# Sum of squares of the first RMSNorm: summed by VectorE, multiplied once with ones, in a kernel for a hybrid decoder layer

## The reference, cut to what matters

```
def rms_norm(x, g):
    y = xf * lax.rsqrt(jnp.mean(xf * xf, axis=-1, keepdims=True) + EPS)
    return (y * g.astype(jnp.float32)).astype(x.dtype)
...
h = rms_norm(xp, g_mix[l])
q, k, v, qi, ki, wi, p, ga, gb = project(h, w_in[l])
```

## Time and profile before

| | us |
|---|---|
| median of 3 runs | 1686.36 |
| lowest, highest | 1683.05, 1686.56 |
| profiled execution, its own time | 1681.07 |
| span of its trace | 1679.6 |
| TensorE busy in the span | 1620.0 (96%) |
| VectorE, ScalarE, GpSimd busy | 599.3, 303.6, 204.9 |

### The profile page before, as it was taken

How to read it: one execution, slowest core, us unless ns; L and a number is a source line. 1 busy time by engine, 2 the same in 40 slices (tenths; PEclk the granted TensorE clock), 3 DMA queues, 4 the chain that set the end, 5 groups by cost and what they waited for, 6 DMA issues and landing times. The chain is left out here.

```text
span 1679.6 us, 33459 instructions
## 1 busy us (share of the span) xinstructions
PE 1620.0 (96%) x13803; PEld 767.0 (46%) x13803; DVE 599.3 (36%) x1168; ACT 303.6 (18%) x617; POOL 204.9 (12%) x267
## 2 busy tenths in 40 slices
PE   7999999999999599999999999999999999999995
PEld 6678577786755233333333333333333333333331
DVE  3409837702323432333233323332333233323333
ACT  1300020006312012111111121111111211121112
POOL 3612400005200000000000000000000000000000
PEclk9899999999999699999999999999999999999996
DMA  4553754722272399999999999999999999999963
GB/s 167 186 169 125 259 198 163 244 78 114 68 298 96 144 375 404 398 399 387 404 391 399 391 401 394 398 384 399 393 400 386 403 395 400 389 399 392 396 248 112
DMA packets 70504, 510.00 MB, mean 304 GB/s; under 512 B 11310, under 2 KB 11758, under 8 KB 45230
## 3 DMA queue, kind: packets, MB, share of 16 engines
q1 hardware_dynamic: 60070, 485.28, 72.9%
q0 software_dynamic: 10384, 24.06, 6.1%
HBM read 491.61 MB, written 22.37 MB: 306 GB/s over the span
## 5 line engine op out<-in xcount | busy, mean ns | idle before, releaser
L1160 PE MATMUL PS<-weight_ring,region_experts 128*32 128x512 f32 x6144 | 680.5, 595 | 2.9 <-issue 1.7
L1160 PEld LDWEIGHTS PS<-weight_ring,region_experts 128*32 128x32 f32 x6144 | 198.7, 110 | 415.4 <-issue 412.0
L822 PE MATMUL PS<-region_x,region_w 128*128 128x260 f32 (+1 forms) x1056 | 240.7, 388 | 2.2 <-ACT region_x L657 1.0
L1167 PE MATMUL PS<-weight_ring,act_turned 128*32 128x512 f32 x2048 | 232.2, 594 | 0.0
L822 PEld LDWEIGHTS PS<-region_x,region_w 128*128 128x128 f32 x1056 | 200.7, 191 | 39.0 <-issue 4.1
L1462 DVE TENSOR_TENSOR region_experts<-region_experts,region_x 128x640 bf16<-128x640 f32 x33 | 27.2, 825 | 397.2 <-DMA region_experts<-b_gu 396.8
L1167 PEld LDWEIGHTS PS<-weight_ring,act_turned 128*32 128x32 f32 x2048 | 63.3, 110 | 137.7 <-issue 134.0
L608 POOL DMA_INDIRECT y_acc<-region_x,idx_i x32 | 46.7, 1460 | 640.6 <-issue 640.6
L1173 PE MATMUL PS<-weight_ring,act_turned 128*32 128x256 f32 x2048 | 122.2, 379 | 0.0
L1173 PEld LDWEIGHTS PS<-weight_ring,act_turned 128*32 128x32 f32 x2048 | 66.6, 110 | 71.2 <-issue 38.3
L592 POOL DMA_INDIRECT region_x<-h_rows,idx_i x33 | 33.4, 1013 | 440.7 <-DVE idx_i L1476 427.6
(11 more groups left out here) (254 smaller groups left out, 1242.1 us busy)
## 6 DMA issues: line engine op xcount, KB each, us to landing
weight_ring<-w_gu SPq DMA_DIRECT2D x128, 2048.0 KB, 13.9
weight_ring<-w_down SPq DMA_DIRECT2D x64, 2048.0 KB, 16.5
region_w<-w_mt SPq DMA_DIRECT2D x33, 512.0 KB, 4.3
weight_ring<-cache_kT SPq DMA_DIRECT2D x64, 256.0 KB, 4.0
weight_ring<-cache_v SPq DMA_DIRECT2D x64, 256.0 KB, 4.0
weight_ring<-w_out SPq DMA_DIRECT2D x2, 2048.0 KB, 11.1
weight_ring<-bias_strip SPq DMA_DIRECT2D x1, 2560.0 KB, 12.6
region_x<-xT SPq DMA_DIRECT2D x4, 536.0 KB, 7.1
```

Source lines behind the costliest of these rows:

```text
L822: mm = pe.matmul(PB[j % 2][:, a, 0:width], lhs(k), rhs(k)[:, width * a:width * a + width], start=(k == 0), stop=(k == nk - 1))
L1160: mm = pe.matmul(out[GRP * j:GRP * j + GRP], hTe[:, k, GRP * g:GRP * g + GRP], weights(c)[:, k, :], start=(k == 0), stop=(k == KD - 1))
L1167: pe.matmul(bank(3)[GRP * j:GRP * j + GRP], actT[:, k, GRP * g:GRP * g + GRP], w_dn[:, k, 512 * q:512 * q + 512], start=(k == 0), stop=(k ...
```

## The change

VectorE adds the eight tiles of sq into one tile ss of 128 x 536 (seven additions), each pair of additions right behind the two xw products of the same pair of tiles. TensorE multiplies ones with ss alone (two products instead of 16), into PSUM banks 4 and 5 (SS) instead of PB[0]. It is no job any more: all job numbers fall by one, so qi0 is job 0. ScalarE computes one root of a 1-column tile right after its squares, so that its table for the root is loaded then. TensorE does twelve products ones x ones into bank 7 before anything else. Item 4 is issued ahead of SP's wait for hT, item 5 ahead of the value weights.

```
--- before.py
+++ after.py
@@ -153,6 +153,7 @@
 
         x_in = part(X1, 0, KD, NT)
         sq = part(X2, 0, KD, NT)
+        ss = part(W6, slot(4) + 1024, NT)
         hT = part(X1, 0, KD, NT)
         xw = part(W6, slot(3), KD, NT)
 
@@ -272,6 +273,7 @@
         DB = [AB[0], AB[1], PSF[:, 0:1024], PSF[:, 1024:2048]]
         PTB = [bank(2), bank(3)]
         RX = bank(1)
+        SS = PS[:, 4:6, :]
         PTR = [PSF[32 * n:32 * n + META, 5 * 512:5 * 512 + P] for n in range(2)]
         L_g = [bank(4, 256), bank(5, 256)]
         L_n = [bank(6, 1)[0:32], bank(7, 1)[0:32]]
...
@@ -300,10 +302,10 @@
         scat = [sem(f"scattered{n}") for n in range(2)]
 
 
-        J_SS, J_QI, J_KI, J_WI, J_K, J_Q, J_P, J_V, J_MIX, J_GATE = 0, 1, 5, 6, 7, 11, 15, 19, 24, 28
+        J_QI, J_KI, J_WI, J_K, J_Q, J_P, J_V, J_MIX, J_GATE = 0, 4, 5, 6, 10, 14, 18, 23, 27
 
         zq_v = zq[:, 0:1032].rearrange("p (c x) -> p c x", x=258)
-        J_A, J_WO = 52, 60
+        J_A, J_WO = 51, 59
 
         N_MT = 17
         ITEMS = N_MT + 3 * KD + KD
@@ -367,10 +369,12 @@
             sp.dma_start(bias_new, bias_n).then_inc(S["small_in"], 16)
             sp.dma_start(cst[:, :], consts).then_inc(S["cst_in"], 16)
             sp.wait_ge(S["small_in"], 80)
+            item(4)
             sp.wait_ge(S["h_done"], KD)
             sp.dma_start(stT, stateT).then_inc(S["stT_in"], 16)
+            item(5)
             sp.dma_start(w_v_sb, w_v).then_inc(S["wv_in"], 16)
-            for n in range(4, 9):
+            for n in range(6, 9):
                 item(n)
             sp.dma_start(strip, bias_strip).then_inc(S["strip_in"], 16)
             sp.wait_ge(S["dots_ready"], len(DOTS))
@@ -639,9 +643,9 @@
                     act.wait_ge(x_full[k // 2], 16)
                 act.activation(sq[:, k, :], x_in[:, k, :], ACT.Square).then_inc(S["sq_done"], 1)
             act.wait_ge(S["eps_set"], 1)
-
-            act.wait_ge(S["proj_done"], 2)
-            nc.scalar.activation(halves(KI[:, :]), wide(0), ACT.Sqrt, bias=eps_t, scale=1.0 / D).then_inc(S["act_taken"], 1)
+            act.activation(spare, eps_t, ACT.Sqrt).then_inc(S["warm_set"], 1)
+            act.wait_ge(S["ss_ready"], 1)
+            nc.scalar.activation(halves(KI[:, :]), SS[:, :, 0:HALF], ACT.Sqrt, bias=eps_t, scale=1.0 / D).then_inc(S["rms_set"], 1)
             act.wait_ge(S["act_taken"], J_QI + 4)
             take(J_KI, halves(wiT[0:H]), wide(J_KI)[64:64 + H]).then_inc(S["wiT_in"], 1)
             act.activation(halves(kiT[0:64]), wide(J_KI)[0:64], ACT.Copy)
@@ -836,6 +840,9 @@
             def hq(k):
                 return hT[:, k, META:NT]
 
+            pe.wait_ge(S["ones_set"], 1)
+            for _ in range(12):
+                pe.matmul(bank(7, P), ones[:, :], ones[:, :], start=True, stop=True)
             pe.wait_ge(w_full[0], 16)
             for k in range(KD):
                 pe.wait_ge(S["xg_done"], k + 1)
@@ -844,12 +851,10 @@
             mm.then_inc(S["proj_done"], 1)
             used[0] = 1
 
-            pe.wait_ge(S["ones_set"], 1)
-            pe.wait_ge(S["sq_done"], KD)
+            pe.wait_ge(S["sq_sum"], KD - 1)
             for a in range(2):
-                for k in range(KD):
-                    mm = pe.matmul(PB[0][:, a, 0:HALF], ones[:, :], sq[:, k, HALF * a:HALF * a + HALF], start=(k == 0), stop=(k == KD - 1))
-            mm.then_inc(S["proj_done"], 1)
+                mm = pe.matmul(SS[:, a, 0:HALF], ones[:, :], ss[:, HALF * a:HALF * a + HALF], start=True, stop=True)
+            mm.then_inc(S["ss_ready"], 1)
 
             for c in range(1, 4):
                 project(J_QI + c, w, xq, KD, width=HQ)
@@ -1244,16 +1249,23 @@
                 if k % 2 == 0:
                     dve.wait_ge(x_full[k // 2], 16)
                 dve.tensor_scalar(xw[:, k, :], x_in[:, k, :], gmix_sb[:, k:k + 1], None, ALU.mult).then_inc(S["xg_done"], 1)
+                if k % 2:
+                    dve.wait_ge(S["sq_done"], k + 1)
+                    if k == 1:
+                        dve.tensor_tensor(ss, sq[:, 0, :], sq[:, 1, :], ALU.add).then_inc(S["sq_sum"], 1)
+                        continue
+                    for m in (k - 1, k):
+                        dve.wait_ge(S["sq_sum"], m - 1)
+                        dve.tensor_tensor(ss, ss, sq[:, m, :], ALU.add).then_inc(S["sq_sum"], 1)
             dve.memset(pT[:, :, 0:PAD], 0.0)
             dve.memset(pool_a[:, 0:PAD], 0.0)
             dve.memset(pool_b[:, 0:PAD], 0.0).then_inc(S["pool_pad"], 1)
 
-            dve.wait_ge(S["act_taken"], 1)
+            dve.wait_ge(S["rms_set"], 1)
             L(dve.reciprocal(KI[:, :], KI[:, :]))
-            dve.wait_ge(S["sq_done"], KD)
             dve.wait_ge(S["xg_done"], KD)
             for c in range(4):
-                dve.wait_ge(S["proj_done"], 2 + c if c else 2)
+                dve.wait_ge(S["proj_done"], c + 1)
                 o = PB[(J_QI + c) % 2][:, :, 0:HQ]
                 inv = KI[:, META:NT].rearrange("p (a b) -> p a b", a=2)
                 dve.tensor_tensor(qiT[:, c, META:NT].rearrange("p (a b) -> p a b", a=2), o, inv, ALU.mult).then_inc(S["act_taken"], 1)
```

More of the change, by code:

```diff
@@ L288, in build_step @@
         pool_done pool_may pool_pad proj_done psT_ready ps_norm pt_ready pt_taken ptz_done pv_pair rank_ready
[L289 to L292, removed]
+        relu_done rms_set round_done router_ready row_ms rsumT_ready rsum_set s_ready sel_ready sidx_taken
+        sig_done slot5_set slot_ready slots_moved small_in smask_done sq_done sq_sum ss_ready stT_in strip_in
+        sums_ready turned unused_done up_full vnew_in vtail_out warm_set wblk_done wcol_in wiT_in wi_out
+        wo0_in wo1_in wv_in xg_done xn_in xt_ready y_ready zero_rows zi_set zq_done zq_zero ztmp_in""".split()
         S = {n: sem(n) for n in names}
```

## The result

The changed kernel takes 1674.4 us, the median of 4 runs (1671.4 to 1676.47); the kernel before 1686.34, the median of 4 (1683.05 to 1686.56). The ratio is 0.994, with a 95% interval of 0.9927 to 0.9954: 10 us less, 7.8 to 12.3. (The two medians themselves lie 11.9 apart, inside that interval.) The profiled execution took 1671.4 us with a span of 1669.5, which is 10.1 less than the span before.

The account below looks back on a forecast made before the run. TensorE, busy 1620.0 of 1679.6 us, was taken as the bound. Gains of 0.8 + 6.3 + 2.1 + 0.3 = 9.5, by the followed course 9.6, gave 1686.36 - 9.6 = 1676.8 us, range 1670 to 1682.

Parts of the forecast that it names:

- Sum of squares: TensorE's products with ones before the query blocks: two products instead of 16, 0.9 us instead of 7.39, gain 6.3 us.
- The gap: TensorE's 2.14 us wait for ScalarE's root before qi1: goes whole with the sum in its own banks, gain 2.1 us.
- qi0 and the clock: First product block: 0.8 us gained if dummies raise the clock by 7.67 us, otherwise 0.
- Rival A: At qi0: dummies don't hold the clock up, or additions starve qi0; 0 to 0.8 us less, 1677.6 us; chance 0.15.
- Items 4 and 5: Loads issued earlier by SP: ki's 0.33 us wait for its weight goes, gain 0.3 us.
- Additions: VectorE's seven additions of sq tiles: 0.75 us each, 5.2 us in all, done at 16.4, almost exactly at qi0's end.
- Dummies: Twelve products ahead of qi0: 24 instructions beside their weight loads, 1.1 to 6.7 us at half clock, costing nothing.
- Downstream: Everything from ki on moves forward by 9.6 us; zi has 13 us to spare and item 9 holds.
- Rival B: Gain hidden elsewhere: zi, gathered index keys or item 9 set the blocks; 1683.4 us with all but 3 lost; chance 0.08.
- The clock later: Fall to 0.50 around the first key block: costs the same when moved forward, or varies from -2.3 to +2.3 us.
- Rival C: Experts' gathers meet the weight stream worse by 0.5 us per expert: 5.9 us slower, 1692.3 us; chance 0.03.
- the one for the start of the sum: Sign in TensorE's timeline: the sum's two products show x4 in about 0.9 us, starting between 16.2 and 17.2 us.

Follow-up runs that it names:

- ones16: The changed kernel with the sum of squares again by 16 products, into the new banks, without the additions on VectorE: 1679.27 us, ratio 0.9968 to the kernel before.
- wait_root: The changed kernel with qi1 waiting for the root again and without the early table: 1677.5 us in one run.
- no_early_table: The changed kernel without the one-column root behind the squares, so the table is loaded when the root is due: 1673.62 us in one run.
- items_late: The changed kernel with items 4 and 5 back behind the wait for hT and the value weights: 1677.01 us in one run.
- dummies20: The changed kernel with 20 dummy products instead of 12: 1674.78 us, ratio 0.9942 to the kernel before.
- xw_first: The changed kernel with xw tiles 4 to 7 ahead of the last four additions and the sum's two products inside qi1: 1675.6 us, ratio 0.9936.
- own_banks_qi2: The changed kernel with 20 dummies, six additions behind all xw tiles, the sum's products inside qi1, qi2 in its own banks: 1672.94 us, ratio 0.9937.

## Why the prediction was right

The forecast was 9.6 us and 1676.8; measured were 10.1 in the span and 1674.4 in the median. The likeliest case came, for the reasons given in the main; the terms, one by one:

- *Sum of squares*: forecast 6.3, shown 6.29 (ones16 against the changed kernel).
- *The gap*: forecast 2.1, shown 2.30 (wait_root, both with the late table). What was late next had 1.9 us to spare by the forecast, and in the trace qi0 is taken by 21.56 and qi2 is due at 16.38 + 21.20/3 = 23.45, 1.9 again. That the early table buys nothing by itself is shown by no_early_table.
- *qi0 and the clock*: forecast 0.8 or nothing, shown 0.88 where the clock holds; in ones16, where it fell back, qi0 was still 0.67 shorter than in the kernel before. Rival A's mechanism is real: of the runs with twelve dummies two fell back after standing 1.95 and 2.00 us; those that stood 1.55 us or less did not. The profiled execution's qi0 ended earlier than forecast (15.44, not 16.3) mainly because its rows landed 0.71 us earlier.
- *Items 4 and 5*: forecast 0.3 against the kernel before, in the table 0.59, of which 0.33 is the old wait. The forecast wait without the move was 39.4 - 38.6 = 0.8; items_late shows 1.32. The 39.4 was itself wrong by 0.6: 24.4 + 0.70 + 2.59 is 27.7 for the end of hT and not 28.3, which would have left a wait of 0.2. In the run the value weights were issued at 27.79 and item 4 was there at 39.06, 11.3 us later and not 10.7, and ki was due 1.0 earlier than forecast. The 0.8 came near by luck.
- *Additions*: forecast 0.75 each, shown 1.47 for two; seven of them end at 15.3, right at the end of qi0, and stretch it, by 0.8 us at the landing of dummies20.
- *Dummies*: 24 instructions were to end at 6.7 by the half clock; they end at 5.9, and at 5.4 to 6.6 in the other traces. They lie beside their weight loads, as taken.
- *Downstream*: ki 10.88 earlier, first expert 10.82. Rival B didn't come. The sample products that need zi start at 100.22, behind the end of GpSimd's copies (86.15) and SP's release (87.39). But the stretch from there to the first expert is not as fixed as the two profiled executions make it look (457.35 and 457.44 us). In five traces of changed kernels (ones16, dummies20, wait_root, xw_first, own_banks_qi2) it takes 460.2 to 460.5, with the same waits. All agree to 0.02 us up to 278.18 us behind its start; then the lower clock lasts longer in the five, in two places. The changed kernel, and under it dummies20, from the same product to the same in each:

```profile
378.40:429.59 51.19, 49.81 (x429) 31.30 (x429) 20.14 (x74) 37.96 (x132) 26.88 (x31) 0.97 0.17 72
...
378.89:431.64 52.75, 51.39 (x428) 32.36 (x428) 20.12 (x74) 38.02 (x132) 26.88 (x31) 0.94 0.17 70
```

  That is 1.56 us of the 3; the rest comes in the routing stage (9.0 against 10.2 to 10.6 us). 3 us are a third of the gain. Whether the change makes the longer course likelier isn't known: the kernel before has two traces, both with the short one.
- *The clock later*: forecast 0, within 2.3 either way. The score products with the gap behind them take 22.20 and 22.22 us, the key blocks 31.14 and 31.17. In the other traces of changed kernels without dummies in that stage they take 22.2 to 23.8 and 30.9 to 32.0.
- *The experts*: 0.68 us longer, 0.02 per expert. Rival C's place moved, at a fifteenth of what it needed to decide. In the other traces of changed kernels this stretch has 1074.95 to 1077.15 us, in those of the kernel before, with and without dummies, 1075.28 and 1075.29; what sets it was not tried.

The Trainium skill, TensorE: Matmul & The Clock Gate, "Part 1: The HAM clock gate", has the rise depend on the execution. The traces agree: the same 24 dummy instructions, begun at 1.12 us, take 4.78 us in one execution of the changed kernel and 5.44 in the other, and 4.32 in wait_root. That it is the clock is read from the rate alone: a window ahead of the first rise shows 1.00 whatever the rate, as the earlier trace rows does.

That 10.1 and 9.6 lie so near is in part luck. ki came 10.88 us earlier, 1.28 more than forecast: 0.71 of it is the rows' landing in this one execution, the rest is in the terms, a little each (0.99 for 0.8 at qi0, 2.30 for 2.1 in the gap, 0.59 for 0.3 with the items). The stretches behind ki then took 0.7 back. All of it is smaller than what one execution differs from another. The median, taken from the runs' median of before, was 2.4 too high. That median of three was itself high: in the later rounds the kernel before had 1685.13, 1684.3 and 1683.23. And the range is narrower than its own terms: 1676.8 + 4 + 2.3 + 0.8 is 1683.9, not 1682.

Of the signs, the one for the start of the sum (16.2 to 17.2) was missed by the profiled execution (15.44) and met by the second one (16.32). None of those for being wrong came: no wait on VectorE is longer than 0.81 us, none stands behind qi0, and qi2 doesn't wait.

## What to carry to other kernels

A reduction over partitions by products with ones costs TensorE as much per tile as a real product (7.23 us for the 16 here, as a key block of the same form): where another engine stands in gaps between landing tiles, sum the tiles there and multiply once. Give such a side result a PSUM bank outside the rotation, so that no product waits for its reader, and when work moves forward, move the loads it needs with it (1.48 us here, against 0.33 of wait visible before). Dummy products for the clock paid in full here where TensorE stood 1.55 us or less between the last of them and the first real product, and not after 1.95 and 2.00; and they pay only in stages in which TensorE truly has nothing to do: look at the engine's spacing, not at the clock, to tell.

## What was not expected of the hardware

The first weights (512 KB, issued at 1.8 us among rows and other items) landed anywhere from 5.96 to 8.22 us, and the second pair of rows from 8.23 to 9.52, with the same issues ahead of them. And standing for about 2 us right behind busy work was followed by a stretch at the lower clock in three executions (ones16, xw_first, the dummies in the kernel before), but not behind the same 2.14 us in the kernel before and in wait_root. Which of the two comes is not settled by these runs.
